# The first stage by halves of the tokens, and the rotary sines taken later, in a hybrid decoder trunk on one core

## The reference, cut to what matters

```python
u = rmsnorm(h, ln1_g[l]); proj = u @ w_in[l]          # 2720 columns, split among four head groups
# A: latent attention with a rotary key     B: causal conv + RG-LRU recurrence
# C: stick-breaking attention               D: HGRN2 gated linear recurrence
h = h + concat(groups) @ w_out[l]
u = rmsnorm(h, ln2_g[l])
h = h + (silu(u @ w_gate[l]) * (u @ w_up[l])) @ w_down[l]
```

## Time and profile before

| | us |
|---|---|
| median of 3 runs | 2534.33 (2533.99 to 2534.8) |
| the profiled execution | 2533.72 |
| its span | 2531.8 |
| TensorE busy | 2486.1 (98%) |
| VectorE busy | 1637.0 (65%) |
| ScalarE busy | 925.7 (37%) |
| GpSimd busy | 954.5 (38%) |
| mean granted TensorE clock | 0.996 |
| decay stages open at | 56.0, 156.9, 1295.3, 1396.7 |

### The profile page before, as it was taken

One profiled execution on the slowest core, in us unless ns is written; L12 is line 12 of the kernel. 1 busy time (PEld: TensorE's weight loads), 2 busy tenths in 40 slices (PEclk: granted clock), 3 DMA queues, 4 the chain that ended last, 5 costly groups with the idle time before them and its releaser, 6 DMA issues.

```text
span 2531.8 us, 32060 instructions
## 1 busy us (share of the span) xinstructions
PE 2486.1 (98%) x12772; PEld 1974.3 (78%) x12772; DVE 1637.0 (65%) x1773; ACT 925.7 (37%) x1342; POOL 954.5 (38%) x531
## 2 busy tenths in 40 slices
PE   7999999999999999999999999999999999999998
PEld 6777776777888888888877777667878888888887
DVE  6887358558766666655677763865696666665554
ACT  6354136634433333100234341565353333331003
POOL 2000320425654555433520014022465455445333
PEclk9999999999999999999999999999999999999999
DMA  5111210042322222522220111002322222234221
GB/s 184 34 43 18 50 30 2 1 150 67 100 92 75 83 92 75 200 100 100 100 68 9 52 34 38 17 1 87 106 75 92 75 83 92 75 121 162 100 100 67
DMA packets 208293, 193.22 MB, mean 76 GB/s; under 512 B 31249, under 2 KB 180881, under 8 KB 208146
## 3 DMA queue, kind: packets, MB, share of 16 engines
q1 hardware_dynamic: 208146, 191.17, 23.3%
HBM read 147.11 MB, written 44.04 MB: 75 GB/s over the span
## 4 chain that ended last, share of the span: by engine, by line
PE 91%; DVE 6%; ACT 1%; issue 1%; DMA 0%; POOL 0%; SPq 0%; DVEq 0%; ACTq 0%
PE ps L242 42%; PE ps L2053 31%; PE ps L1469 3%; PE ps L1446 3%; PE ps L684 2%; PE ps L1458 2%; PE ps L1917 2%; PE ps L1427 1%; DVE u_lo L298 1%; DVE u_t L2529 1%; PE ps L775 0%; PE ps L770 0%; PE ps L1505 0%; PE ps L1174 0%; DMA w_raw<-w_up 0%
## 5 line engine op out<-in xcount | busy, mean ns | idle before, releaser
L2172 DVE TENSOR_TENSOR h<-ps,h 128x1024 f32<-128x1024 f32 x176 | 214.7, 1223 | 196.7 <-PE ps L242 195.5
L2014 POOL TENSOR_TENSOR w_a<-w_raw,w_a 128x512 fp32r<-128x512 f32 x110 | 177.7, 1624 | 319.1 <-ACT w_a L2004 319.1
L242 PE MATMUL ps<-u_hi,w_hi 128*128 128x512 f32 x864 | 283.3, 409 | 5.5 <-DVE u_lo L298 4.3
L242 PE MATMUL ps<-u_lo,w_hi 128*128 128x512 f32 x864 | 267.5, 391 | 0.0
L242 PE MATMUL ps<-u_hi,w_lo 128*128 128x512 f32 x864 | 267.2, 390 | 0.0
L2053 PE MATMUL ps<-u_b,w_a 128*128 128x512 f32 x1056 | 255.2, 391 | 6.3 <-POOL w_a L2014 6.3
L2053 PE MATMUL ps<-u_t,w_s 128*128 128x512 f32 x1056 | 247.2, 389 | 1.7 <-POOL w_s L2014 1.6
L2053 PEld LDWEIGHTS ps<-u_b,w_a 128*128 128x128 f32 x1056 | 198.8, 188 | 48.5 <-POOL w_a L2014 7.2
L2053 PEld LDWEIGHTS ps<-u_t,w_s 128*128 128x128 f32 x1056 | 198.0, 188 | 43.7 <-POOL w_s L2014 2.5
L242 PE MATMUL ps<-hidden_lo,down_hi 128*128 128x512 f32 x640 | 197.1, 389 | 0.0
L242 PE MATMUL ps<-hidden_hi,down_hi 128*128 128x512 f32 x640 | 197.0, 389 | 0.0
(11 more groups left out here) (383 smaller groups left out, 4879.5 us busy)
## 6 DMA issues: line engine op xcount, KB each, us to landing
w_raw<-w_gate SPq DMA_DIRECT2D x44, 512.0 KB, 3.7
w_raw<-w_up SPq DMA_DIRECT2D x44, 512.0 KB, 4.8
hidden_spill<-hidden_gate SPq DMA_DIRECT2D x44, 512.0 KB, 2.6
w_raw<-w_down SPq DMA_DIRECT2D x44, 512.0 KB, 4.4
hidden_back<-hidden_spill SPq DMA_DIRECT2D x44, 512.0 KB, 4.1
w_raw<-w_in SPq DMA_DIRECT2D x42, 512.0 KB, 3.8
h_spill<-h SPq DMA_DIRECT2D x32, 512.0 KB, 4.1
h<-h_spill SPq DMA_DIRECT2D x32, 512.0 KB, 8.4
```

What stands on the lines that cost most here:

```text
L242: last = nc.tensor.matmul(ps[:, bank0 + half, :], a, b[:, half * HALF:(half + 1) * HALF], start=(k == order[0] and n == 0), stop=(k == ord ...
L2014: nc.gpsimd.tensor_tensor(lo, src, hi.bitcast(F32), ALU.subtract).then_inc(w_lo, 1)
L2172: nc.vector.tensor_tensor(wide(h[:, m, :]), pair(p), wide(h[:, m, :]), ALU.add)\
```

## The change

In the setup stage everything up to the two products works by halves of 512 tokens. The range reduction's first step (positions times frequency) comes right after the position matmul, which now follows tokens 0 and 1; its other steps come last on VectorE. Transposed tokens go to bank pairs 1, 2, 3 in turn. VectorE copies tokens 5 and 7, ScalarE the other six. The high and low parts of the first half of the tokens are formed while tokens 6 and 7 are still missing, and these two are transposed inside slot 0's product for the first half, before k = 1 and k = 3. The order of products is: slot 0 first half, slot 1 first half, slot 0 second half, slot 1 second half; the row-scale matmul stands before the last k of the last one. The clamped angles are kept in `RT`. The sines are taken by ScalarE in the first decay stage, between the exponentials of levels 4 and 5, and the sign is put into the frequency table. The table set with both Ln and Exp is loaded once at the start of setup. In all four decay stages ScalarE now splits slot 3 before its first Abs, and VectorE before its log-sigmoid.

```diff
+        DVE_TOKENS = (5, 7)
+        def token_pair(t):
+            return 1 + t % 3
+        def written(engine, t):
+            if t in DVE_TOKENS:
+                engine.wait_ge(h_copied, DVE_TOKENS.index(t) + 1)
+            else:
+                engine.wait_ge(h_written, sum(n not in DVE_TOKENS for n in range(t + 1)))
# VectorE, setup
+            def low_part(m, half):
+                dve.wait_ge(norm0[2], KT * half + m + 1)
+                nc.vector.scalar_tensor_tensor(half_of(ulo, m, half), half_of(h, m, half), ln1(m),
+                                               half_of(uhi, m, half).bitcast(F32), ALU.mult, ALU.subtract)
+            dve.wait_ge(pos_done, 1)
+            turn(nc.vector.tensor_scalar(wide(AN[:, :]), pair(0, slice(0, 64)), CO[0:64, K_FREQ:K_FREQ + 1],
+                                         None, ALU.mult))
+            low_part(0, 0)
+            low_part(1, 0)
+            token_part(5)
+            low_part(2, 0)
+            low_part(3, 0)
+            token_part(7)
+            for m in range(4, KT):
+                low_part(m, 0)
+            for m in range(KT):
+                low_part(m, 1)
...
-            for m in range(KT):
-                norm_dve(dve, norm0, m, uhi[:, m, :], ulo[:, m, :], ln1(m))
-            (range reduction, then the wait for x_rs and the diagonal, then the sign)
+            (the wait for x_rs and the diagonal, then the rest of the range reduction)
# ScalarE, setup
+            for t in range(4):
+                token_part(t)
+            written(act, 3)
+            high_part(0, 0)
+            high_part(1, 0)
+            token_part(4)
+            high_part(2, 0)
+            high_part(3, 0)
+            token_part(6)
+            for m in range(4, KT):
+                high_part(m, 0)
+            all_written(act)
             for m in range(KT):
-                nc.scalar.activation(uhi[:, m, :], h[:, m, :], ACT.Copy, scale=ln1(m)).then_inc(norm0[2], 1)
+                high_part(m, 1)
             for t in range(TT):
                 (squares of x, as before)
# TensorE, setup
+            def first_half(k):
+                if k in (1, 3):
+                    tokens(6 + k // 2)
+                pe.wait_ge(norm0[3], k + 1)
+            def last_steps(k):
+                if k == KT - 1:
+                    pe.wait_ge(slot_split, 3)
+                    pe.wait_ge(rs_diag, 1)
                     (row-scale matmul)
+            for t in range(2):
+                tokens(t)
+            (position matmul)
+            for t in range(2, 6):
+                tokens(t)
+            half_product(0, 0, first_half)
+            half_product(1, 0, lambda k: None)
+            all_written(pe)
+            half_product(0, 1, second_half).then_inc(next_done, 1)
+            half_product(1, 1, last_steps).then_inc(left, 1)
             third_ahead(pe, 2)
# decay stages, ScalarE
                 exp_and_ln()
+                slot_hi(3)
                 act.wait_ge(bank_free[0], 1)
                 (Abs, Exp, Ln of bF)
-                slot_hi(3)
...
                 level_exp(4)
+                if (l, pr) == (0, 0):
+                    sines(act)
                 level_exp(5)
# decay stages, VectorE
                 read(1, bQ[:, :])
+                slot_lo(3)
                 dve.wait_ge(bank_free[0], 1)
                 dve.wait_ge(f_soft, 3)
...
-                slot_lo(3)
                 dve.wait_ge(logf_ready, 1)
```

More of the change, by code:

```diff
@@ L69 @@
 LB_A, LB_C, LB_D, LB_C1 = 0, 1, 2, 3
-K_ID, K_NEGS, K_NEGC, K_HEADS, K_FREQ, K_SIGN, K_N = 0, 128, 256, 384, 512, 513, 514
+K_ID, K_NEGS, K_NEGC, K_HEADS, K_FREQ, K_N = 0, 128, 256, 384, 512, 513
 TWO_PI_1 = 6.28125
@@ L341, in build, with all_written, half_of, token_copy @@
         RK = at_r("turns", 88, [64, S])
+        DVE_TOKENS = (5, 7)
[6 more added lines that the diff above has]
+                engine.wait_ge(h_written, sum(n not in DVE_TOKENS for n in range(t + 1)))
+        def all_written(engine):
+            written(engine, TT - 2)
+            written(engine, TT - 1)
+        def half_of(t, k, half):
+            return t[:, k, half * HALF:(half + 1) * HALF]
+        def token_copy(t):
+            return h[:, :, t * P:(t + 1) * P], pair(token_pair(t)).rearrange("p b (k t) -> p (b k) t", t=P)
         def setup_sp_part(sp):
@@ L355, in setup_sp_part @@
             load_third_slot(sp, 0)
-            sp.wait_ge(h_written, TT)
+            all_written(sp)
             for k in range(KT):
@@ L422, in turn, with token_part @@
                 dve.wait_ge(rope_step, r)
+            def low_part(m, half):
+                dve.wait_ge(norm0[2], KT * half + m + 1)
+                nc.vector.scalar_tensor_tensor(half_of(ulo, m, half), half_of(h, m, half), ln1(m),
+                                               half_of(uhi, m, half).bitcast(F32), ALU.mult, ALU.subtract)\
+                    .then_inc(norm0[3], 1)
+            def token_part(t):
+                to, at = token_copy(t)
+                dve.wait_ge(proj_done, t + 1)
+                nc.vector.tensor_copy(to, at).then_inc(h_copied, 1)
+            dve.wait_ge(pos_done, 1)
[11 more added lines that the diff above has]
+                low_part(m, 1)
             c = 0
@@ L445, in setup_dve_part @@
             lam_next(nc.vector.tensor_scalar(lbt[:, 3, :], v(4), -LRU_C, None, ALU.mult))
-            for m in range(KT):
-                norm_dve(dve, norm0, m, uhi[:, m, :], ulo[:, m, :], ln1(m))
-            dve.wait_ge(pos_done, 1)
-            turn(nc.vector.tensor_scalar(wide(AN[:, :]), pair(2, slice(0, 64)), CO[0:64, K_FREQ:K_FREQ + 1],
-                                         None, ALU.mult))
+            dve.wait_ge(x_rs, 2)
+            nc.vector.tensor_tensor(
+                RD[:, :, :], XMS[:, :].rearrange("p (t o) -> p t o", o=1).broadcast_to([P, TT, P]),
+                ident.rearrange("p (o c) -> p o c", o=1).broadcast_to([P, TT, P]), ALU.mult).then_inc(rs_diag, 1)
             turn(nc.vector.tensor_scalar(RK[:, :], AN[:, :], 1.0 / (2 * math.pi), ROUND, ALU.mult, ALU.add))
@@ L456, in setup_dve_part @@
                 turn(nc.vector.scalar_tensor_tensor(AN[:, :], RK[:, :], -part, AN[:, :], ALU.mult, ALU.add))
[L457 to L465, removed]
+            turn(nc.vector.tensor_scalar(RT[0:64, :], AN[:, :], PI_BELOW, -PI_BELOW, ALU.min, ALU.max))
         def setup_act_part(act):
+            exp_and_ln()
             act.wait_ge(small_loaded, 96)
@@ L476, in setup_act_part, with token_part, high_part @@
             nc.scalar.activation(LW[:, 7:10, :], LW[:, 7:10, :], ACT.Ln).then_inc(ready0, 1)
-            for t in range(TT):
+            def token_part(t):
+                to, at = token_copy(t)
                 act.wait_ge(proj_done, t + 1)
[L480 to L483, removed]
+                nc.scalar.activation(to, at, ACT.Copy).then_inc(h_written, 1)
+            def high_part(m, half):
+                nc.scalar.activation(half_of(uhi, m, half), half_of(h, m, half), ACT.Copy, scale=ln1(m))\
+                    .then_inc(norm0[2], 1)
+            for t in range(4):
[10 more added lines that the diff above has]
+            all_written(act)
             for m in range(KT):
-                nc.scalar.activation(uhi[:, m, :], h[:, m, :], ACT.Copy, scale=ln1(m)).then_inc(norm0[2], 1)
+                high_part(m, 1)
             for t in range(TT):
@@ L497, in setup_act_part, with sines @@
             nc.scalar.activation(wide(RS[:, :]), pair(3), ACT.Copy).then_inc(rs_part, 1)
-            act.wait_ge(rope_step, 7)
-            nc.scalar.activation(RK[0:32, :], AN[0:32, :], ACT.Abs).then_inc(act_step, 1)
+        def sines(act):
+            nc.scalar.activation(RT[0:32, :], RT[0:32, :], ACT.Abs).then_inc(act_step, 1)
             act.wait_ge(act_step, 1)
-            nc.scalar.activation(RT[0:32, :], RK[0:32, :], ACT.Sin, scale=-1.0,
-                                 bias=half_pi[0:32, 0:1]).then_inc(ready0, 1)
-            nc.scalar.activation(RT[32:64, :], AN[32:64, :], ACT.Sin).then_inc(ready0, 1)
+            nc.scalar.activation(RT[0:32, :], RT[0:32, :], ACT.Sin, scale=-1.0,
+                                 bias=half_pi[0:32, 0:1]).then_inc(act_step, 1)
+            nc.scalar.activation(RT[32:64, :], RT[32:64, :], ACT.Sin).then_inc(act_step, 1)
+            exp_and_ln()
         def setup_pe_part(pe):
@@ L508, in setup_pe_part, with tokens, half_product, second_half @@
             pe.wait_ge(ready0, 3)
[L509 to L514, removed]
+            def tokens(t):
                 pe.wait_ge(x_loaded[t], 16)
-                if t >= 2:
-                    pe.wait_ge(h_written, t - 1)
+                if t >= 3:
+                    written(pe, t - 3)
                 for k in range(KT):
-                    b = 2 * (t % 2) + k // 4
-                    last = nc.tensor.transpose(ps[:, b, (k % 4) * P:(k % 4 + 1) * P],
```

(45 more changed lines are left out.)

## The result

The changed kernel takes 2557.1 us (median of 4 runs, 2548.5 to 2558.3), against 2534.3 before: a ratio of 1.0085, interval 1.0073 to 1.0098. It is slower by 22.8 us where 12 were forecast. The profiled execution took 2557.53, its span 2555.5 at a mean granted clock of 0.989.

A forecast was written before the change was run, and what follows sets the result against it. The prediction took the chain of waits, 91% on TensorE, as the bound. Terms of -0.8 (first decay stage), +8.9 (later stalls), +1.7 and +2.5 (clock) summed to +12.3 us, forecasting 2546.3 us, range 2538.5 to 2551.

The forecast's parts named there:

- The slot's delay: Decay-stage openings: ScalarE waits for slot 3's weights, so level 0 comes late; +8.9 us over the second to fourth stages.
- Setup by halves: Setup stage: opening at 51.7 instead of 56.0, but level 0 of the first decay stage only 0.8 us earlier.
- The earlier split gains nothing where TensorE is concerned: Decay-stage opening: slot 3 was ready about when TensorE wanted it, so at most a wait under 0.2 us is saved.
- The contention with GpSimd: End of setup: VectorE's range-reduction steps collide with GpSimd's split of the third slot, taken as 4 us.
- The sines: First decay stage, before the level-5 exponential: 5.8 us of work covered by 10.37 us of idle time, so no cost.
- The clock: TensorE after the four stalls: low granted clock costs +1.7 us after the first and 2.5 for the three others.
- rival B: TensorE at the decay stages: all four stalls drop the clock, +14.9 us, 2549; chance 0.20.
- Rival D: Decay-stage openings: slot 3's wait on ScalarE is hidden, the last three stages lose nothing, 2529; chance 0.05.

The follow-up runs named there:

- experiment 1: The changed kernel with slot 3's split put back to its old place in all four decay stages; 2530.5 us, 0.9986.
- experiment 2: The kernel before with only slot 3's split moved to the opening of the decay stages; 2561.7 us, 1.0126.
- experiment 5: The changed kernel with only slot 3's low part (VectorE) put back to its old place, the high part still first on ScalarE; 2550.2 us, 1.0066.
- experiment 7: The changed kernel with slot 3's weights requested before the first, second and fourth decay stages open, and the old order in the third; 2535.2 us, 1.0007.
- experiment 6: The kernel before with only the sines moved to the first decay stage and the sign put into the frequencies; 2533.6 us, 0.9998.
- experiment 3: The changed kernel with unread 512-column matmuls filling TensorE's stall before level 0, 22 in the first decay stage, 14 in the others; 2545.0 us, 1.0045.
- experiment 10: The changed kernel itself, unchanged, on another chip and with more runs; 2555.8 us, 1.0098.
- experiment 4: The changed kernel with the score matmuls of levels 0 and 1 in two groups instead of 8 before each k; 2545.3 us, 1.0045.
- experiment 9: The changed kernel with 16 unread 512-column matmuls in each decay stage right behind TensorE's wait for level 0; 2566.0 us, 1.0128.

## Why the prediction was wrong

The direction and the mechanism held; one term of the sum was mis-sized.

- *The slot's delay* held: Abs at 5.05 behind the opening (forecast 5.2), stalls of 5.2, 3.4, 2.7, 3.4 (5.4, 3.1, 2.6, 3.2). Experiments 1 and 2 show that the slot's new place carries the whole loss, 26.6 us by 2557.1 against 2530.5, and experiment 5 that ScalarE's part alone brings the stalls. Experiment 7 shows that most of it is the wait for the landing: with the weights there, three stages stall for 4.1 us instead of 12.0, and 4.7 of the 26.6 us are left. The split's own time ahead of the Abs is the rest.
- *Setup by halves* held to within 1 us: TensorE idle 1.28 before k = 4 (1.3), its last setup product done at 48.9 (48.0), VectorE's clamp last, opening 52.35 (51.7), level 0 at 76.01 (75.4). The step "The earlier split gains nothing where TensorE is concerned" was not right with the earlier opening: in experiment 1 TensorE waits 1.6 us for slot 3's low part in the first stage. The contention with GpSimd was as forecast: two light steps of 0.69 took 2.38 and 2.76.
- *The sines* held: three operations and two table loads ran from 99.48 to 105.4, and the level-5 exponential behind them still waited 4.61 us on VectorE.
- *The clock* failed, in the step "one drop after the 5.4 us stall (+1.7), and half a drop for each of the three others (+0.85 each, 2.5)". It priced a drop at 3.4 us of low clock, read from two places of the trace before, and so 4.2 us in all. All four stalls dropped the clock, and the drops cost 14 to 16 us in the first trace. The length of 3.4 us was that of one trace: at the first of these places, the start of slot 0's product, the traces of experiments 2 and 6 have 5.8 and 5.4 us of work at the low clock. Those places, like those of experiment 5, are followed by long matmuls. Behind level 0's wait stand six long matmuls between every eight short score matmuls, and there a low clock lasted from 3.3 to 17 us of work. Where no span is long the change costs 14 to 16 us, near rival B's 14.9: the trace of 2549.4 has 4.6 and three times 3.4 us behind its stalls, and the runs of 2548.5 and 2549 lie inside the range of 2538.5 to 2551.
- Rival B (all four drop) was right on the number of drops and still too low (2549), for the same reason. Rival D, the faster one, fell by the 2.79 us for which ScalarE waited on the DMA.

Shown is that idle time starts the low clock (experiment 3) and that its length varies in this place from run to run (2 and 10). That the score matmuls between the long ones hold it down is argued, not shown. Experiments 4, 5 and 9 support it, each with shorter spans and a smaller spread (2.5 to 4.2 us against 9.8 to 21.5), but in experiment 4 one span still held 8.3 us. The spans of 5.7 to 6.2 us ahead of long matmuls alone (experiment 5) are nearly as long as the third stage's 6.8, so only the span of 17 us stands clearly apart, and one trace has it. What decides, run by run, whether a span lasts 3 or 17 us stays open.

## What to carry to other kernels

Work put at a stage's opening must have its data there: a split that waits for a transfer requested at the same moment holds everything behind it on an engine that executes in order, here 3.8 us for a slack of 0.4. Ask the slack of the consumer, not the share of the engine that is delayed. Price a stall on TensorE with the work that follows it: a gap of 3 us ahead of uniform long matmuls costs itself and, as half of the 3.3 to 6.2 us of work seen at the low clock, some 1.6 to 3.1 us; ahead of a mix with short ones it cost up to 8. Give such a term a range and not one trace's value.

## What the runs showed that I had not expected

The low granted clock can last 17 us with TensorE busy all the time (17.16 of 18.00 us, clock 0.53), and the same program then differs by 15 us between runs (2549 and 2564) where the kernel before differs by 3.5. Filling a stall with useless matmuls saved 12 us. Nor does the clock need a gap to fall: near the end of the changed kernel, behind a run of matmuls of one column without a gap, it fell at 2538.4 and stayed low for 6.5 us of work.

```profile
2536.00:2538.00 2.00, 2.00 (x20) 2.00 (x19) 0.00 (x0) 0.00 (x0) 0.00 (x0) 1.00 0.00 0
...
2539.00:2545.00 6.00, 5.76 (x26) 5.46 (x27) 3.87 (x6) 4.26 (x9) 0.00 (x0) 0.50 0.30 121
```
